# The half swap of the rotary embedding in a hybrid decoder layer: from a matrix product to transfers issued by GpSimd

## The chip, the cores and the metric

The kernel runs on one core of one Trainium2 chip. The metric is the device time of one launch in microseconds. The kernel before took 1616.17 us (median of 3 runs, 1615.53 to 1617.78).

## The reference

One decoder layer over 512 tokens of width 1024: a combined input projection, then two mixing parts side by side (differential attention with a rotary embedding, and an RWKV-7 time mixing), an output projection, and a mixture of experts (top 4 of 32). What matters here is the rotary embedding. Each attention head has two 64-wide parts for the queries and the keys, and each part is turned by an angle per position:

```python
def apply_rope(x, cos, sin):
    c = cos[:, :, None, None, :]
    s = sin[:, :, None, None, :]
    x1, x2 = jnp.split(x.astype(F32), 2, axis=-1)
    return jnp.concatenate([x1 * c - x2 * s, x2 * c + x1 * s], axis=-1).astype(x.dtype)

q = apply_rope(q.reshape(B, S, DA_HEADS, 2, DA_HEAD_DIM), cos, sin)
k = apply_rope(k.reshape(B, S, DA_HEADS, 2, DA_HEAD_DIM), cos, sin)
s = jnp.einsum('bhcqd,bhckd->bhcqk', qi, kt, preferred_element_type=F32) * scale
```

The second term of each half needs the other half of the same vector: 32 values are exchanged with the 32 beside them.

## The kernel before

The program has three parts: `front` (input projection and mixing, up to about 377 us), `output_and_route`, and `experts`. Only `front` is touched. There the features lie on the 128 partitions and the 512 tokens along the free dimension, so that a swap of halves is an exchange of partition blocks: rows 0 to 31 with 32 to 63, and 64 to 95 with 96 to 127.

`front` writes one instruction stream for each engine. The order of each is written out by hand, and engines wait for one another by counting semaphores: `s_out` counts projected tiles that ScalarE has copied to SBUF, and the classes `Steps` (objects `PE`, `AC`, `DV`) count named steps of TensorE, ScalarE and VectorE. The lists `MIX_PE`, `MIX_ACT` and `MIX_DVE` name these steps in order, so a step that is taken out of a stream is taken out of its list.

The mixing loop runs four times, for `j` in 0 to 3, once for each attention head and the pair of RWKV heads beside it; one pass is called a head below. `own_tiles(j)` gives the number `n0` of its first projected tile: tile `n0` holds the queries, `n0 + 1` the keys, `n0 + 2` the values. Beside its mixing, TensorE projects the next head's tiles in pieces (`tile`, L784), except in the last head. What lies around the swap:

- SP (L319) loads weight tiles of 512 KB; each waits for VectorE's split of an earlier one.
- ScalarE copies query and key tiles into `pall` (L384, L467 and L469 of the loop), copies `kappa` and `beta` (L472, L475), and splits a weight tile (L375).
- TensorE computes the products of `beta`, `kappa` and `khat` (L842, L845, L853), the first level products (L861), then the swap: two products with a constant matrix `swap` into banks 7 and 6 (L899, L900). Directly behind it come the level updates (L870, L873), a piece of the next tile, and the level products of level 1 (L861).
- VectorE masks the level products (L658), computes one product for the bonus (L673), the sign on the sine table in head 0 only (L677), the products with the cosines (L680), adds the level update (L666, twice), splits a weight tile except in the last head (L536), then computes the products with the sines from the two banks into `sc` (L686), masks level 1 (L658) and adds the two parts (L690).
- GpSimd computes the angles and writes an empty list to memory (L366) at the beginning; after that it has no work until `front` ends.

`sc` also holds the exponentials of the attention scores (L435) and, in its first columns, squares of the output (L447).

Of the kernel before, what the change touches and what calls it, by code (L numbers as in the profile page):

```python
# [23 lines left out]
ALU = mybir.AluOpType  # L24
# [3 lines left out]
P = 128  # L28
D = 1024
S = 512  # L30
NT = S // P
KT = D // P
IN_TILES = 26
HEADS = 4
CH = 64
# [96 lines left out]
def build_program(nc, d, out):  # L132
    _, at = constant_tables()
    with ExitStack() as top:
# [28 lines left out]
        with ExitStack() as st:  # L163
            front(nc, d, sb, sem, st, dict(cst=cst, cols=cols, stat=stat, o_t=o_t, list_dram=list_dram), con, ident, psum, bank)
# [20 lines left out]
def own_tiles(j):  # L185

    return LEAD + 6 * j


def place_of(n):  # L190
# [1 line left out]
    return n if n < 2 else ORDER[n] // HEADS  # L192


MIX_PE = (["lora_w", "lora_a", "kk_sum", "lora_g", "mb", "t_kappa", "t_beta", "t0_0", "t0_1", "mk", "rope_swap", "x0_0", "x0_1"]
# [19 lines left out]
def front(nc, d, sb, sem, st, g, con, ident, psum, bank):  # L215
# [7 lines left out]
    s_whi, s_wlo, s_prod, s_out = sem("w_hi"), sem("w_lo"), sem("projected"), sem("p_copied")  # L223
    s_zero, s_rope, s_lam1, s_ang = sem("p_zeroed"), sem("rope_steps"), sem("lam_steps"), sem("angles_done")
    s_trig, s_lex, s_lora, s_set, s_set2 = sem("trig_done"), sem("lam_exp"), sem("lora_loaded"), sem("mix_set"), sem("mix_set2")
    s_ready = sem("lora_inputs_ready")
    s_empty, s_emptied = sem("empty_lists_ready"), sem("slot_lists_emptied")
    s_rest, s_part_out = sem("less_and_masks_ready"), sem("own_parts_copied")
    PE = Steps(sem("mix_tensor_steps"), MIX_PE)
    AC = Steps(sem("mix_scalar_steps"), MIX_ACT)  # L230
    DV = Steps(sem("mix_vector_steps"), MIX_DVE)

    pall = sb(st, "pall", [P, 6, S + 1])
    cosb = sb(st, "cosb", [P, S])
    sinb = sb(st, "sinb", [P, S])
# [38 lines left out]
    sc = sb(st, "sc", [P, 2, S])  # L274
# [22 lines left out]
    def tile_of(group, shift=1):  # L297
        return pall[:, group, shift:shift + S]
# [25 lines left out]
    @block.gpsimd  # L324
    def _(pool):
        nc.gpsimd.dma_start(cols[:], d["cols"]).then_inc(s_cols, 16)
        nc.gpsimd.dma_start(posi[:], d["positions"].to_broadcast([P, S])).then_inc(s_pos, 16)
        nc.gpsimd.dma_start(lam[:].rearrange("p a b -> p (a b)"), d["lam"].to_broadcast([P, 256])).then_inc(s_lam, 16)
        nc.gpsimd.memset(zz[:, 0, :], 0.0)
        nc.gpsimd.memset(pe_[:, :, 0:1], 1.0)  # L330
        nc.gpsimd.memset(pall[:, :, 0:1], 0.0).then_inc(s_zero, 1)
        pool.wait_ge(s_zero, 1)

        pool.wait_ge(s_cst, 16)
        pool.wait_ge(s_pos, 16)
        step = 0

        def chain(ins):
            nonlocal step
            step += 1  # L340
            ins.then_inc(s_rope, 1)
            pool.wait_ge(s_rope, step)

        two_pi = 2 * np.pi
        c1 = 6.28125
        c2 = float(np.float32(two_pi - c1) - np.float32(two_pi - c1) % np.float32(2.0 ** -20))
        c3 = float(two_pi - c1 - c2)
        chain(nc.gpsimd.tensor_copy(cosb[:], posi[:]))
        chain(nc.gpsimd.tensor_scalar(sinb[:], cosb[:], con("inv"), None, ALU.mult))
        for dst, shift in ((ang, 0.25), (turns, 0.0)):  # L350

            chain(nc.gpsimd.tensor_scalar(cosb[:], sinb[:], float(1 / two_pi), shift, ALU.mult, ALU.add))
            chain(nc.gpsimd.tensor_scalar(cosb[:], cosb[:], 12582912.0, None, ALU.add))
            chain(nc.gpsimd.tensor_scalar(cosb[:], cosb[:], 12582912.0, None, ALU.subtract))
            for c, angle in ((c1, sinb[:]), (c2, dst[:]), (c3, dst[:])):
                chain(nc.gpsimd.tensor_scalar(taken, cosb[:], -c, None, ALU.mult))
                chain(nc.gpsimd.tensor_tensor(dst[:], taken, angle, ALU.add))
            if shift:
                chain(nc.gpsimd.tensor_scalar(dst[:], dst[:], float(np.pi / 2), None, ALU.add))
            chain(nc.gpsimd.tensor_scalar(dst[:], dst[:], 3.1415925, -3.1415925, ALU.min, ALU.max))  # L360
            pool.sem_inc(s_ang, 1)
        nc.gpsimd.memset(empty, 0.0).then_inc(s_empty, 1)
        pool.wait_ge(s_empty, 1)
        nc.gpsimd.memset(empty[:, :, 0:1], BIG).then_inc(s_empty, 1)
        pool.wait_ge(s_empty, 2)
        nc.gpsimd.dma_start(g["list_dram"].rearrange("(p r) w -> p r w", p=P), empty).then_inc(s_emptied, 16)  # L366
        pool.wait_ge(s_emptied, 16)

    @block.scalar
    def _(act):  # L370
# [162 lines left out]
    def _(dve):  # L533
        def split(n):
            dve.wait_ge(s_whi, n + 1)
            nc.vector.tensor_tensor(w_lo[:, n % 3], w_raw[:, n % 2], w_hi[:, n % 3].bitcast(F32), ALU.subtract).then_inc(s_wlo, 1)  # L536
# [35 lines left out]
        for j in range(HEADS):  # L572
            more = j < HEADS - 1
            n0 = own_tiles(j)
# [106 lines left out]
            level_added(0)  # L681
            if more:
                split(n0 + 3)
            dve.wait_ge(PE.sem, PE.reached(j, "rope_swap"))
            for a, group, dst in rope:
                nc.vector.tensor_tensor(sc[:, group, :], bank(7 - group), sinb[:], ALU.mult).then_inc(DV.sem, DV.step(a + "s"))  # L686
            level_masked(1)
            own("ks")
            for a, group, dst in rope:
# [75 lines left out]
    def _(pe):  # L765
# [27 lines left out]
        for j in range(HEADS):  # L793
            more = j < HEADS - 1
            n0 = own_tiles(j)
# [5 lines left out]
            def dv(name):  # L801
                pe.wait_ge(DV.sem, DV.reached(j, name))

            def ac(name):
                pe.wait_ge(AC.sem, AC.reached(j, name))

            def scores(i):
                n = (i + 1) * P
                for c in range(2):
                    rows = slice(64 * c, 64 * c + 64)  # L810
                    nc.tensor.matmul(bank(6 + c, 0, n), qr[rows, i * P:(i + 1) * P], kro[rows, 0:n], start=True, stop=False)
                for c in range(2):
                    last = nc.tensor.matmul(bank(6 + c, i * P, n), masks[:, 0, :], masks[:, 1, :], start=False, stop=True)
                last.then_inc(PE.sem, PE.step(f"score{i}"))
# [79 lines left out]
            level_products(0, (1,))  # L894
            dv("khat")
            quarters(from_k).then_inc(PE.sem, PE.step("mk"))
            pe.wait_ge(s_out, n0 + 2)
            ac("e_beta")
            nc.tensor.matmul(bank(7), con("swap"), tile_of(0), start=True, stop=True)  # L899
            nc.tensor.matmul(bank(6), con("swap"), tile_of(1), start=True, stop=True).then_inc(PE.sem, PE.step("rope_swap"))  # L900
            level_update(0, 0)
            level_update(0, 1)
            tile(n0 + 2, 2, 5)
# [2 lines left out]
            level_update(1, 1)  # L906
            tile(n0 + 2, 5, 8)
            dv("k")
            scores(0)
            pe.wait_ge(s_out, n0 + 3)  # L910
            turned("v_turn", 4 + (n0 + 2) % 2, lambda t: pall[:, 2, t * P + 1:t * P + P + 1])
# [34 lines left out]
            for h in range(2):  # L946
                for t in range(NT):
                    u = h * NT + t
                    for rows in halves:
                        last = nc.tensor.matmul(bank(2, u * CH, (u + 1) * CH, rows), ak[rows, h, t, 0, :], vt[rows, t, halves[h]],  # L950
                                                start=True, stop=True)
# [5 lines left out]
            for h in range(2):  # L957
                for t in range(NT):
                    for rows in halves:
                        last = nc.tensor.matmul(bank(3 * (1 - h), t * P, t * P + P, rows), xx[rows, h, t, 1, :], rh[rows, h, t, :],  # L960
                                                start=True, stop=True)
# [11 lines left out]
            for t in range(NT):  # L973
# [4 lines left out]
                for h, hs, c, tok in each:  # L978
                    last = nc.tensor.matmul(bank(c, 256 + t * CH, 320 + t * CH, hs), bn[tok, t, hs], wu[tok, h, t, CH:P],
                                            start=False, stop=True)  # L980
# [42 lines left out]
            for t in range(NT):  # L1023
                for h, hs, c, tok in each:
                    last = nc.tensor.matmul(bank(c, t * CH, (t + 1) * CH, hs), zz[hs, 2 * t + c, :], qt[hs, t, tok],
                                            start=False, stop=t == NT - 1)
# [1073 lines left out]
```

## Time and profile before

| | before |
|---|---|
| median of 3 runs | 1616.17 us |
| profiled execution | 1614.44 us |
| its span | 1612.8 us |
| mixing, one whole head | 82 us |
| end of `front` | about 377 us |
| TensorE busy over the span | 1553.0 us (96%) |
| VectorE busy | 1321.4 us (82%) |
| ScalarE busy | 1069.4 us (66%) |
| GpSimd busy | 315.3 us (20%) |

The profile records one execution. PE is TensorE (PEld its weight loads), DVE is VectorE, ACT ScalarE, POOL GpSimd, SP the sync engine. L899 is line 899 of the kernel. An entry "out<-in" names the tensors that an instruction writes and reads, and "[idle before <-releaser]" gives the time for which its engine had nothing to do before it, and the event that ended that. The busy times of TensorE are modelled at their ends: matmuls are pipelined and records overlap, so the cadence is read from starts. The engines' totals cover all stages; the swap lies in one of them, and is read from that stage's own rows.

### The profile page before, as it was taken

What the parts mean: (1) busy time and instruction counts of PE and PEld (TensorE: products, weight loads), DVE (VectorE), ACT (ScalarE), POOL (GpSimd) and SP (SyncE); (2) the same over time, 40 slices, a digit from 0 to 9 for tenths busy, and PEclk for the clock granted to TensorE, in tenths of its full rate; (3) what the DMA queues carried; (4) which work ended last, traced back from release to release, by engine and by line L of the source; (5) the groups of instructions that cost most, each with busy time, mean ns of one, the idle gap of its engine ahead of it and who ended that gap; (6) DMA issues with size and microseconds to landing.
All of it is one profiled execution on the core that took longest, in us unless ns stands there. A gap on an engine that the chain in (4) does not pass through costs nothing.

```text
span 1612.8 us, 27293 instructions
## 1 busy us (share of the span) xinstructions
PE 1553.0 (96%) x10213; PEld 1257.3 (78%) x10214; DVE 1321.4 (82%) x1098; ACT 1069.4 (66%) x1011; POOL 315.3 (20%) x262
## 2 busy tenths in 40 slices
PE   5999999987989999999999999999999999999996
PEld 4677777775868888888888888888888888888885
DVE  5556656555499999999999999999999999999996
ACT  4635353434367877777777777777777777777774
POOL 6200000000145312211211222122222112212210
PEclk9999999997989999999999999999999999999998
DMA  6110101005399999999999999999999999999992
GB/s 191 50 54 27 54 28 44 12 2 200 136 363 388 363 389 382 385 382 380 379 376 372 384 390 375 376 368 375 376 377 384 387 375 372 376 362 384 381 377 112
DMA packets 98189, 463.21 MB, mean 287 GB/s; under 512 B 11136, under 2 KB 37792, under 8 KB 48848
## 3 DMA queue, kind: packets, MB, share of 16 engines
q1 hardware_dynamic: 86032, 429.59, 67.9%
q0 software_dynamic: 12096, 32.75, 7.7%
q8 instruction: 45, 0.74, 0.2%
q14 instruction: 16, 0.13, 0.0%
HBM read 448.51 MB, written 22.69 MB: 292 GB/s over the span
## 4 chain that ended last, share of the span: by engine, by line
PE 74%; DVE 1%; DMA 1%; issue 0%; ACT 0%; DVEq 0%; POOLq 0%
PE psum L1919 29%; PE psum L1922 14%; PE psum L1947 14%; PE psum L1952 7%; PE psum L1317 3%; PE psum L1901 2%; PE psum L1909 2%; PE psum L1935 1%; DVE w_pieces_lo L1741 0%; DMA xg<-h_rows,gath_i 0%; PE psum L2037 0%; PE psum L1333 0%; PE psum L1325 0%; DVE x L1863 0%; DMA w_pieces<-in_w_out 0%
## 5 line engine op out<-in xcount | busy, mean ns | idle before, releaser
L1741 DVE TENSOR_TENSOR w_pieces_lo<-w_pieces,w_pieces_hi 128x2048 fp32r<-128x2048 f32 x384 | 867.3, 2286 | 79.9 <-ACT w_pieces_hi L1605 79.8
L1605 ACT ACTIVATE w_pieces_hi<-w_pieces 128x2048 fp32r<-128x2048 f32 x384 | 736.2, 1919 | 220.7 <-PE psum L1922 156.7
L1919 PE MATMUL psum<-w_pieces_hi,xh 128*128 128x512 f32 x1024 | 284.5, 400 | 0.0
L1919 PE MATMUL psum<-w_pieces_hi,xl 128*128 128x512 f32 x1024 | 274.4, 390 | 0.0
L1922 PE MATMUL psum<-w_pieces_lo,xh 128*128 128x512 f32 x1024 | 274.2, 389 | 0.0
L1919 PEld LDWEIGHTS psum<-w_pieces_hi,xl 128*128 128x128 f32 x1024 | 192.3, 188 | 41.3
L1922 PEld LDWEIGHTS psum<-w_pieces_lo,xh 128*128 128x128 f32 x1024 | 192.2, 188 | 40.2
L1919 PEld LDWEIGHTS psum<-w_pieces_hi,xh 128*128 128x128 f32 x1024 | 185.5, 189 | 45.1 <-issue 11.3
L1545 POOL DMA_INDIRECT sum_rows<-ys,this_i x30 | 114.5, 3815 | 423.8 <-ACT ys L1625 423.5
L1947 PE MATMUL psum<-w_pieces_hi,ah 128*128 128x512 f32 x512 | 158.0, 390 | 0.1
L1947 PE MATMUL psum<-w_pieces_hi,al 128*128 128x512 f32 x512 | 157.7, 389 | 0.0
L1952 PE MATMUL psum<-w_pieces_lo,ah 128*128 128x512 f32 x512 | 136.8, 389 | 0.0
L1947 PEld LDWEIGHTS psum<-w_pieces_hi,al 128*128 128x128 f32 x512 | 96.1, 188 | 20.0
L1952 PEld LDWEIGHTS psum<-w_pieces_lo,ah 128*128 128x128 f32 x512 | 96.1, 188 | 20.0
L1947 PEld LDWEIGHTS psum<-w_pieces_hi,ah 128*128 128x128 f32 x512 | 95.8, 188 | 20.2 <-DVE al L1757 0.5
L784 PE MATMUL psum<-h_hi_sb,w_hi_sb 128*128 128x512 f32 x208 | 88.0, 423 | 0.0
L1535 POOL COPY this_f<-slot_lists_sb 128x1 f32 x30 | 27.7, 922 | 299.3 <-DMA sum_rows<-ys,this_i 295.2
L784 PE MATMUL psum<-h_hi_sb,w_lo_sb 128*128 128x512 f32 x208 | 81.5, 392 | 0.0
L784 PE MATMUL psum<-h_lo_sb,w_hi_sb 128*128 128x512 f32 x208 | 81.3, 391 | 0.0
L1609 ACT ACTIVATE xh<-psum 128x512 fp32r<-128x512 f32 x64 | 37.6, 588 | 41.8 <-PE psum L1901 41.8
L1128 POOL DMA_DIRECT2D w_pieces<-in_ffn_norm_w x1 | 0.6, 554 | 326.1 <-POOLq L163 326.1
L384 ACT ACTIVATE pall<-psum 128x512 f32<-128x512 f32 x14 | 8.3, 595 | 73.4 <-PE psum L784 73.4
(369 smaller groups left out, 1915.1 us busy)
## 6 DMA issues: line engine op xcount, KB each, us to landing
w_pieces<-in_mlp_w SPq DMA_DIRECT2D x384, 1024.0 KB, 7.9
w_raw<-in_w_in SPq DMA_DIRECT2D x26, 512.0 KB, 4.0
w_pieces<-in_w_out SPq DMA_DIRECT2D x8, 512.0 KB, 9.1
sum_rows<-x POOLq DMA_DIRECT2D x5, 512.0 KB, 3.7
chunk_work<-in_x SPq DMA_DIRECT2D x4, 512.0 KB, 5.6
x<-in_x SPq DMA_DIRECT2D x4, 512.0 KB, 13.6
h_rows<-w_pieces POOLq DMA_DIRECT2D x4, 512.0 KB, 3.5
x<-sum_rows POOLq DMA_DIRECT2D x4, 512.0 KB, 11.5
```

Of the source, the lines that this page charges most:

```text
L784: last = nc.tensor.matmul(o, w[:, n % 3, k, :], h[:, k, :], start=k == 0 and m == 0, stop=k == KT - 1 and m == 2)
L1317: last = nc.tensor.matmul(bank(2 * t + c), o[:, k, t * P:(t + 1) * P], w[:, k, c * 512:(c + 1) * 512], start=k == 0 and m == 0, stop=k == ...
L1545: nc.gpsimd.indirect_dma_start(sum_dram, bass.IndirectOffsetOnAxis(this_i[:, 0:1], 0), ys[:], None, compute_op=ALU.add).then_inc(s_scat, 16)
L1605: nc.scalar.activation(hi[:, p % RING], raw[:, raw_slot(b, p)].rearrange("p r n -> p (r n)"), ACT.Copy).then_inc(s_hi, 1)
L1609: nc.scalar.activation(xh[:, 4 * q:4 * q + 4, :].rearrange("p a b -> p (a b)"), bank(from_bank), ACT.Copy).then_inc(s_xh, 1)
L1741: nc.vector.tensor_tensor(lo[:, p % RING], raw[:, raw_slot(b, p)].rearrange("p r n -> p (r n)"), hi[:, p % RING].bitcast(F32), ALU.subtrac ...
L1901: last = nc.tensor.transpose(bank(into, k * P, k * P + P), xg[:, (4 * q + k) * P:(4 * q + k + 1) * P], ident)
L1909: last = nc.tensor.transpose(bank(into, k * P, k * P + P), rows[:, k // 2, k % 2, :], ident)
L1919: nc.tensor.matmul(bank(up_bank(b) + c), a[:, k, :], hi[:, p % RING, c * 512:(c + 1) * 512], start=False, stop=False)
L1922: last = nc.tensor.matmul(bank(up_bank(b) + c), xh[:, k, :], lo[:, p % RING, c * 512:(c + 1) * 512], start=False, stop=k == KT - 1)
L1947: nc.tensor.matmul(bank(into + c), a[:, 2 * p + r2, :], hi[:, p % RING, r2 * D + c * 512:r2 * D + (c + 1) * 512], start=p == 0 and r2 == 0 ...
L1952: last = nc.tensor.matmul(bank(into + c), ah[:, 2 * p + r2, :], lo[:, p % RING, r2 * D + c * 512:r2 * D + (c + 1) * 512], start=False, sto ...
```

## The change

The two products with the swap matrix leave TensorE's stream, and `rope_swap` its list of steps. In their place GpSimd, once per head, waits for the copies of tiles `n0` and `n0 + 1`, and from the second head on for the previous head's last readers of `sc`. It then issues four transfers from `pall` to `sc`, each of 32 partitions by two rows of 512 values, to the partition block beside it. VectorE waits for the count of a new semaphore `s_swapped` instead of TensorE's step, and its products with the sines read and write `sc` in place. TensorE's wait for `e_beta`, which had stood ahead of the swap, now stands ahead of the first scores. GpSimd waits for all transfers at the end.

```diff
-MIX_PE = ([..., "t0_0", "t0_1", "mk", "rope_swap", "x0_0", "x0_1"]
+MIX_PE = ([..., "t0_0", "t0_1", "mk", "x0_0", "x0_1"]
...
+    s_swapped = sem("rope_halves_swapped")
...
         pool.wait_ge(s_emptied, 16)
+        for j in range(HEADS):
+            pool.wait_ge(s_out, own_tiles(j) + 2)
+            if j:
+                pool.wait_ge(DV.sem, DV.reached(j - 1, "a3"))
+                pool.wait_ge(AC.sem, AC.reached(j - 1, f"o_copy{NT - 1}"))
+            for a in range(0, P, CH // 2):
+                b = a ^ (CH // 2)
+                nc.gpsimd.dma_start(sc[a:a + CH // 2, :, :], pall[b:b + CH // 2, 0:2, 1:S + 1]).then_inc(s_swapped, 16)
+        pool.wait_ge(s_swapped, 64 * HEADS)
...
-            dve.wait_ge(PE.sem, PE.reached(j, "rope_swap"))
+            dve.wait_ge(s_swapped, 64 * (j + 1))
             for a, group, dst in rope:
-                nc.vector.tensor_tensor(sc[:, group, :], bank(7 - group), sinb[:], ALU.mult).then_inc(DV.sem, DV.step(a + "s"))
+                nc.vector.tensor_tensor(sc[:, group, :], sc[:, group, :], sinb[:], ALU.mult).then_inc(DV.sem, DV.step(a + "s"))
...
             quarters(from_k).then_inc(PE.sem, PE.step("mk"))
-            pe.wait_ge(s_out, n0 + 2)
-            ac("e_beta")
-            nc.tensor.matmul(bank(7), con("swap"), tile_of(0), start=True, stop=True)
-            nc.tensor.matmul(bank(6), con("swap"), tile_of(1), start=True, stop=True).then_inc(PE.sem, PE.step("rope_swap"))
             level_update(0, 0)
...
             dv("k")
+            ac("e_beta")
             scores(0)
```

## Rows read from the trace of the kernel before

**Rows 1.** Busy time by engine over one whole head, clock, DMA share, GB/s.

```profile
142.00:224.00 82.00, 81.33 (x1131) 61.88 (x1130) 49.15 (x87) 36.12 (x77) 0.00 (x0) 1.00 0.14 40
```

**Rows 2.** Line of the first swap product: duration ns min/median/max, first and last start.

```profile
L899 PE MATMUL psum<-pall,cst x8: 592/644/697, 74.1 to 321.2; 128*128 128x512 f32 x8
```

**Rows 3.** Timeline, TensorE's weight loads, second head: start us, us, instruction, idle before.

```profile
156.32 0.30 PEld L899 LDWEIGHTS psum<-pall,cst 128*128 128x128 f32 x2 [0.17 <-issue]
...
158.24 0.19 PEld L870 LDWEIGHTS psum<-chunk_work 64*64 64x64 f32 x4 [0.76 <-DVE kro L680]
```

**Rows 4.** Timeline of VectorE around the swap in the second head (head 1).

```profile
155.56 0.42 DVE L658 TENSOR_TENSOR chunk_work<-psum,cst 128x256 f32<-128x256 f32 x1 [0.45 <-PE psum L861]
...
157.16 0.69 DVE L680 TENSOR_TENSOR kro<-pall,cosb 128x512 f32<-128x512 f32 x1
159.43 0.69 DVE L666 TENSOR_TENSOR chunk_work<-chunk_work,psum 128x512 f32<-128x512 f32 x1 [1.58 <-PE psum L873]
160.37 0.69 DVE L666 TENSOR_TENSOR chunk_work<-chunk_work,psum 128x512 f32<-128x512 f32 x1 [0.25 <-PE psum L873]
160.97 1.22 DVE L536 TENSOR_TENSOR w_lo_sb<-w_raw,w_hi_sb 128x1024 fp32r<-128x1024 f32 x1
162.11 1.28 DVE L686 TENSOR_TENSOR sc<-psum,sinb 128x512 f32<-128x512 f32 x2
```

**Rows 5.** Timeline of VectorE around the swap in the first head (head 0).

```profile
74.37 0.48 DVE L677 TENSOR_SCALAR sinb<-sinb,cst 128x512 f32<-128x512 f32 x1
...
75.50 0.68 DVE L680 TENSOR_TENSOR kro<-pall,cosb 128x512 f32<-128x512 f32 x1
...
78.18 0.69 DVE L666 TENSOR_TENSOR chunk_work<-chunk_work,psum 128x512 f32<-128x512 f32 x1 [0.25 <-PE psum L873]
...
79.92 1.28 DVE L686 TENSOR_TENSOR sc<-psum,sinb 128x512 f32<-128x512 f32 x2
81.11 0.83 DVE L658 TENSOR_TENSOR chunk_work<-psum,cst 128x256 f32<-128x256 f32 x2
```

**Rows 6.** Timeline of VectorE around the swap in the last head (head 3).

```profile
324.73 0.69 DVE L666 TENSOR_TENSOR chunk_work<-chunk_work,psum 128x512 f32<-128x512 f32 x1 [0.24 <-PE psum L873]
325.34 1.28 DVE L686 TENSOR_TENSOR sc<-psum,sinb 128x512 f32<-128x512 f32 x2
327.62 0.89 DVE L658 TENSOR_TENSOR chunk_work<-psum,cst 128x256 f32<-128x256 f32 x2 [1.00 <-PE psum L861]
```

**Rows 7.** Timeline of ScalarE: the key tile's copy in heads 0, 1 and 3.

```profile
68.06 0.60 ACT L384 ACTIVATE pall<-psum 128x512 f32<-128x512 f32 x1 [2.06 <-PE psum L784]
...
150.25 0.60 ACT L384 ACTIVATE pall<-psum 128x512 f32<-128x512 f32 x1 [2.08 <-PE psum L784]
...
314.62 0.60 ACT L384 ACTIVATE pall<-psum 128x512 f32<-128x512 f32 x1 [2.08 <-PE psum L784]
```

**Rows 8.** Timeline of GpSimd: its last issue in `front`, its first ones afterwards.

```profile
51.31 0.64 POOL L366 DMA_DIRECT2D slot_lists<-o_t  x1 [0.30 <-POOL o_t L364]
...
378.03 0.55 POOL L1128 DMA_DIRECT2D w_pieces<-in_ffn_norm_w  x1 [326.08 <-POOLq L163]
...
379.65 0.53 POOL L1131 DMA_DIRECT2D ffn_norm_cols<-in_ffn_norm_w  x1
```

**Rows 9.** DMA issues of GpSimd: count, KB each, median us from issue to landing.

```profile
xg<-h_rows,gath_i POOLq DMA_INDIRECT x33, 8.3
...
sum_rows<-ys,this_i POOLq DMA_INDIRECT x30, 13.4
...
slot_lists<-o_t POOLq DMA_DIRECT2D x1, 128.0 KB, 3.2
...
ffn_norm_cols<-in_ffn_norm_w POOLq DMA_DIRECT2D x1, 4.0 KB, 7.5
```

**Rows 10.** Timeline of ScalarE: the first head's last use of `sc`.

```profile
125.35 0.36 ACT L447 ACTIVATE sc<-psum,ast 128x128 f32<-128x128 f32 x1
```

**Rows 11.** Line L603 on VectorE: duration ns min/median/max, first and last start.

```profile
L603 DVE SCALAR_TENSOR_TENSOR rkv<-pall,cols,rkv x12: 724/744/894, 49.9 to 307.2; 128x512 f32<-128x512 f32 x12
```

More of the change, by code:

```diff
@@ L192, in place_of @@
     return n if n < 2 else ORDER[n] // HEADS
-MIX_PE = (["lora_w", "lora_a", "kk_sum", "lora_g", "mb", "t_kappa", "t_beta", "t0_0", "t0_1", "mk", "rope_swap", "x0_0", "x0_1"]
+MIX_PE = (["lora_w", "lora_a", "kk_sum", "lora_g", "mb", "t_kappa", "t_beta", "t0_0", "t0_1", "mk", "x0_0", "x0_1"]
           + ["t1_0", "t1_1", "x1_0", "x1_1", "score0", "v_turn"]
```

## The prediction, made before the result was known

> **What bounds the kernel now.** I looked first at the stretches of the mixing stage, because the change touches nothing else. In the 82 us of one whole head TensorE is busy for 81.3 us, VectorE for 49.2 and ScalarE for 36.1, GpSimd for nothing, and the DMA engines for 14% [rows 1]. That is the reading that matters most: in a head TensorE has next to nothing to wait for, so a microsecond taken out of its instruction stream should be a microsecond off the head, unless it hands the path to another engine. GpSimd and the DMA engines, where the work is sent, are free. TensorE's granted clock is 1.00 there, the level of 2.4 GHz, so nothing is lost to the clock that could be won back.
>
> Next I read the order of events around the swap on each engine, in three heads, to learn when its input is ready, when its result is used, and what slack lies between.
>
> **What is removed.** Per head two fp32 products of 128x512. Each shows as two passes: the line of the first product has 8 records over four heads, 592 to 697 ns [rows 2], and the second line is alike. Four such passes would be some 2.4 us, but that is not the saving, because passes overlap. The weight loads give the cadence: in head 1 the first of the swap starts at 156.32 and the first of the level update behind it at 158.24 [rows 3]. So TensorE moves on 1.92 us earlier. The level update's input is ready by then: VectorE's L658 writes it and ends at 155.56 + 0.42 = 155.98 [rows 4]. The note on the row at 158.24 that blames a vector step of the rope is only that of the last event before it; that line of the code waits for nothing of the rope.
>
> **Does VectorE let it through?** Its sequence is: cosine products (L680), first update (L666, twice, each waits for TensorE), the split of a weight tile (L536), sine products (L686), next mask (L658). The cadence of back-to-back 128x512 operations is 0.60 us (L666 at 160.37, L536 at 160.97) [rows 4].
> Head 1: the second L680 starts at 157.16, VectorE is free at 157.76. The first L666 could have its input at 159.43 - 1.92 = 157.51, so it starts at 157.76; the second is free at 158.36, its input comes at 160.37 - 1.92 = 158.45. It starts then, and the full 1.92 us is passed on (with only 0.09 us to spare). Head 2 has the same spacing.
> Head 0 has one more operation (the sign on the sine table), so VectorE is free at 75.50 + 0.60 = 76.10; the two L666 start at 76.10 and 76.70, the second against 78.18 before. Here 78.18 - 76.70 = 1.48 us is passed on, for L686 and L658 follow without a gap (79.92, 81.11) [rows 5]: VectorE, not TensorE, is last at L658.
> Head 3 has no weight split here; its second L666, at 324.73, comes forward by 1.92 as in head 1 [rows 6].
> Sum: 1.48 + 3 x 1.92 = 7.24 us, if the swapped rows are there in time.
>
> **What is added.** GpSimd issues four transfers per head, 32 partitions x 4 KB (128 KB) each, 512 KB in all, once the copy of the second tile is done. VectorE waits for them instead of for TensorE, and queued behind that wait are the sine products, L658 and all further levels, on which TensorE waits in turn. The sine product's form hardly changes: it reads SBUF in place of PSUM, and L680, both operands in SBUF, takes the same 0.69 us as L666 with one in PSUM [rows 4]. I cost that at nothing.
>
> When must the swap have landed? From the end of the second copy (start plus 0.60: 68.66, 150.85, 315.22 [rows 7]) to the brought-forward L686:
> head 0: 79.92 - 1.48 - 68.66 = 9.78 us;
> heads 1 and 2: 162.11 - 1.92 - 150.85 = 9.34 us;
> head 3: 325.34 - 1.92 - 315.22 = 8.20 us, and there L658 had stood idle for 1.00 us waiting for TensorE [rows 6], so 9.20 us.
>
> When does it land? GpSimd is free: its last issue in this stage is at 51.31, and that started 0.30 us after its releaser; consecutive issues lie (379.65 - 378.03) / 3 = 0.54 us apart [rows 8]. I take 0.55, so the fourth is issued at 0.30 + 3 x 0.55 = 1.95 us. From issue to landing no row shows a transfer from SBUF to SBUF. The nearest are 3.2 us for 128 KB out of SBUF in this stage [rows 9], and from above the 7.5 us of the last of four GpSimd issues while the DMA engines were full of other loads [rows 9]. I take 3.2 to 3.5, because the stage's DMA engines are at 14%: a weight load of 512 KB runs beside the first microseconds, no more. So the swap is complete 5.2 to 5.5 us after the copy: 3.8 us to spare at the least. With 7.5 it is 9.45 us: late by 0.11 in heads 1 and 2 and by 0.25 in head 3, half a microsecond in all. The new waits for the previous head's last weights and last output copy cost nothing: that copy ran at 125.35, 25 us before GpSimd needs it [rows 10]. The end wait on GpSimd is over some 50 us before the stage ends. SP's queue is not touched; its loads wait for weight splits, which come forward with the rest. TensorE's wait for the copy of beta moves to just before the scores, many microseconds after that copy.
>
> A rule speaks against the choice of queue. Ahead of the sine product VectorE runs tensor-tensor forms [rows 4]; the only tensor-scalar form is head 0's at 74.37, 5.7 us after that head's copy [rows 5, 7]. The Trainium skill (SBUF — State Buffer, the box "The DVE blocks DMA trap") says that descriptors of a GpSimd DMA cannot be written while VectorE holds the shared port pair in a two-port mode, and that the sync queue is immune; it exempts tensor_tensor. By that rule the sum stays as it is here, and I cannot see it proven by a row.
>
> The Trainium skill (DMA: Bandwidth & Descriptors, "Anatomy of one DMA") fits about 2.0 us plus bytes over 436 GB/s for such a DMA, an estimate of 2.3 us for 128 KB. The measured 3.2 us is used instead.
>
> **The rivals.**
> A. The swap lands late but still pays. If a transfer takes 8.3 us, as the gathers issued by GpSimd do [rows 9], it is complete at 1.95 + 8.3 = 10.25 us: late by 0.47, 0.91, 0.91 and 1.05, together 3.34; gain 3.9 us, 1612.3. For it: the kernel has such landings. Against: those moved scattered rows in a loaded stage. Chance 0.10.
> B. VectorE becomes the bound. It has 0.09 us of spare in heads 1 to 3. If GpSimd's descriptor work stretches VectorE's operations, as L603 ranges from 0.724 to 0.894 us [rows 11], the longest while GpSimd still computed (its arithmetic ends just before 51.31 [rows 8]), then some 11 operations between the copy and the swap's end by 0.17 us each are 1.87, less the 0.45 us for which VectorE waits at L658 anyway [rows 4]: 1.4 us per head. What is left is about 4 x 0.4 = 1.6 us: 1614.6, not to be told from no change. Against: GpSimd's part is four issues, not arithmetic. Chance 0.09.
> C. The four transfers do not overlap: each starts when the one before has landed. Then 0.30 + 4 x 3.2 = 13.1 us, late by 3.32, 3.76, 3.76 and 3.90, together 14.7; less 7.24, 7.5 us slower, 1623.7. The place is VectorE's wait ahead of L686 in each head. It decides against the change from where the lateness sums to 7.24, at 11.2 us after the copy. For it: the transfers share one queue and one semaphore. Against: four GpSimd issues 0.54 us apart, of which the last landed 7.5 us after its own issue [rows 8, 9], which leaves no room for three landings of that length before it. Chance 0.08.
> D. The same wait, but with descriptors held up while VectorE is busy, as long as the 13.4 us of the scatters [rows 9]: 15.35 us, late by 23.7 in all, 16.5 us slower, 1632.7. Against: those scatters ran beside full DMA engines. Chance 0.05.
> That the swap never leaves TensorE is not possible: its products are gone from the stream.
>
> **How the numbers follow.** The likeliest case, chance 0.68, gives 7.24 us. The profiled execution took 1614.44 us (span 1612.8), 1.7 us under the median of the runs, 1616.17; the sum is a difference and is taken from that median: 1616.17 - 7.24 = 1608.9. Its own range is 1607.7 to 1610.5, from TensorE gaining a little more than the cadence (up to 0.3 us per head) to landings of 7.5 us and some stretch. Two in ten may be left out: A and B must come in, C and D stay outside, so 1607.5 to 1616.5 holds 0.87. A measurement of this kernel can tell about 0.2%, 3.2 us, from no change: faster means under 1612.9. The first case and A give 0.78 for faster, B gives 0.09 for the same, C and D 0.13 for slower.
>
> **What the profile of the changed kernel would show.** No products with the swap matrix; the first weight load of the level update directly behind those of khat, and heads about 1.9 us shorter (1.5 in the first). Sixteen GpSimd issues, four per head, 0.55 us apart, starting some 0.3 us after the second copy, each landing in 3 to 4 us. VectorE with no idle time ahead of L686's counterpart; an idle time there, released by a DMA, would show A, C or D, and its length says which. Sine products, or L646 and L649 beside the issues, longer than 0.69 us would show B. TensorE's granted clock should stay at 1.00 in the first three heads. I would be wrong if a transfer between partitions of SBUF is much slower than one out of it, which no row here shows, or if TensorE, freed of 1.9 us, meets a later wait that I have not followed: before, it idled for 0.7 us in 82 [rows 1], so there was none hidden nearby.

## The result and the profile after

The changed kernel took 1607.72 us (median of 5 runs, 1607.04 to 1608.66) against 1616.17 before (5 runs by now, with the same median and range): a ratio of 0.9949, with a 95% interval of 0.9938 to 0.9961, so about 8.2 us faster and between 6 and 10. The forecast was 1608.9, in a range of 1607.5 to 1616.5. The profiled execution took 1607.04 us, span 1605.3 (before: 1614.44 and 1612.8).

The lines of TensorE's weight loads in the second head, which answers to [rows 3] (start us, us, instruction; line numbers are 10 higher in this part):

```profile
155.98 0.25 PEld L863 LDWEIGHTS psum<-kr,khat 64*64 64x64 f32 x6
156.20 0.25 PEld L880 LDWEIGHTS psum<-chunk_work 64*64 64x64 f32 x4
```

The level update's loads stand directly behind those of `khat`: the swap is gone and nothing waits in its place. VectorE in the same head, to be read beside [rows 4]:

```profile
157.25 0.68 DVE L690 TENSOR_TENSOR kro<-pall,cosb 128x512 f32<-128x512 f32 x1
157.85 1.28 DVE L676 TENSOR_TENSOR chunk_work<-chunk_work,psum 128x512 f32<-128x512 f32 x2
159.05 1.22 DVE L546 TENSOR_TENSOR w_lo_sb<-w_raw,w_hi_sb 128x1024 fp32r<-128x1024 f32 x1
160.18 1.28 DVE L696 TENSOR_TENSOR sc<-sc,sinb 128x512 f32<-128x512 f32 x2
```

The idle times of 1.58 and 0.25 us ahead of the two updates are gone, and the sine products (L696) have no idle time ahead of them, so the swap was there. Where it came from, GpSimd's issues in the first, second and last head, and their landings over all 16 (count, KB each, median us from issue to landing):

```profile
70.92 2.18 POOL L376 DMA_DIRECT2D sc<-pall  x4 [19.07 <-ACT pall L394]
...
151.22 2.11 POOL L376 DMA_DIRECT2D sc<-pall  x4 [78.12 <-ACT pall L394]
...
311.58 2.11 POOL L376 DMA_DIRECT2D sc<-pall  x4 [78.07 <-ACT pall L394]
```

```profile
sc<-pall POOLq DMA_DIRECT2D x16, 128.0 KB, 3.8
```

The copies of the key tile, which answer to [rows 7], give the length of a head from start to start:

```profile
69.60 0.60 ACT L394 ACTIVATE pall<-psum 128x512 f32<-128x512 f32 x1 [3.73 <-PE psum L794]
...
150.34 0.60 ACT L394 ACTIVATE pall<-psum 128x512 f32<-128x512 f32 x1 [2.11 <-PE psum L794]
...
230.51 0.60 ACT L394 ACTIVATE pall<-psum 128x512 f32<-128x512 f32 x1 [2.08 <-PE psum L794]
...
310.69 0.60 ACT L394 ACTIVATE pall<-psum 128x512 f32<-128x512 f32 x1 [2.07 <-PE psum L794]
```

| us | before | after | gain |
|---|---|---|---|
| start to the copy in head 0 | 68.06 | 69.60 | -1.54 |
| head 0 to head 1 | 82.19 | 80.74 | 1.45 |
| head 1 to head 2 | 82.17 | 80.17 | 2.00 |
| head 2 to head 3 | 82.20 | 80.18 | 2.02 |
| head 3 to GpSimd's first issue behind `front` | 63.41 | 59.96 | 3.45 |
| together | 378.03 | 370.65 | 7.38 |

The first and the last line hold something that is not the change. In each profile TensorE's granted clock was at 0.5 (1.2 GHz) for one stretch of `front` (leaving out its end, where TensorE idles for 9.8 us in both): in the changed kernel's at 60 us, ahead of anything that was changed, in that of the kernel before at 365 us. The columns of these rows are the stretch, its length, the busy time and instructions of TensorE, its weight loads, VectorE, ScalarE and GpSimd, the granted clock, and the DMA share with GB/s. The first row is of the changed kernel, the second of the one before:

```profile
60.00:63.40 3.40, 3.40 (x7) 1.90 (x6) 1.65 (x3) 3.36 (x6) 0.00 (x0) 0.50 0.00 0
```

```profile
364.60:368.00 3.40, 3.40 (x42) 3.06 (x40) 0.28 (x1) 0.73 (x4) 0.00 (x0) 0.51 0.00 0
```

The one goes with a start that is later by 1.54 us. What the other cost can be read on its own, from the weight loads just ahead of it:

```profile
359.47 0.56 PEld L969 LDWEIGHTS psum<-chunk_work,wu 64*64 64x64 f32 x32 [2.12 <-ACT wu L507]
...
363.68 0.14 PEld L999 LDWEIGHTS psum<-zz,gt 64*64 64x64 f32 x2 [1.76 <-DVE zz L744]
```

The same two loads of the changed kernel start at 353.48 and 357.68. From the key tile's copy in head 3 to the first of them are 44.85 us before and 42.79 after: the last head gains 2.06 us. From the second to GpSimd's first issue are 14.35 and 12.97 us: the stretch at half clock cost 1.4. So the two stretches nearly cancel, and the four heads give 1.45 + 2.00 + 2.02 + 2.06 = 7.5 us. Behind `front` the two profiles differ by another 0.1 us only.

### The profile page after: what moved, and what is told of

The parts are those of the page before. It is cut to its first block, busy times and chain, and to the rows that moved or that the text cites. A ratio compares the mean times of both kernels' runs of the same rounds, so it can differ in the third digit from the quotient of the medians.

```text
span 1605.3 us, 27281 instructions
## 1 busy us (share of the span) xinstructions
PE 1544.0 (96%) x10197; PEld 1253.3 (78%) x10198; DVE 1320.3 (82%) x1098; ACT 1068.9 (67%) x1011; POOL 324.7 (20%) x278
## 4 chain that ended last, share of the span: by engine, by line
PE 74%; DVE 1%; DMA 1%; issue 0%; ACT 0%; DVEq 0%; POOLq 0%
PE psum L1926 29%; PE psum L1929 14%; PE psum L1954 14%; PE psum L1959 7%; PE psum L1324 3%; PE psum L1908 2%; PE psum L1916 2%; PE psum L1942 1%; DVE w_pieces_lo L1748 0%; DMA xg<-h_rows,gath_i 0%; PE psum L2044 0%; PE psum L1340 0%; PE psum L1332 0%; DVE x L1870 0%; DMA w_pieces<-in_w_out 0%
## 5 line engine op out<-in xcount | busy, mean ns | idle before, releaser
L1552 POOL DMA_INDIRECT sum_rows<-ys,this_i x30 | 106.1, 3537 | 421.0 <-ACT ys L1632 420.7
L1542 POOL COPY this_f<-slot_lists_sb 128x1 f32 x30 | 43.7, 1455 | 304.7 <-DMA sum_rows<-ys,this_i 300.4
L376 POOL DMA_DIRECT2D sc<-pall x16 | 8.5, 541 | 253.3 <-ACT pall L394 253.3
```

The costliest lines, as they stand in the source:

```text
L1542: nc.gpsimd.tensor_copy(this_f[:], lists[:, bass.ds(e, 1), 0:1].rearrange("p a c -> p (a c)")).then_inc(s_float, 1)
L1552: nc.gpsimd.indirect_dma_start(sum_dram, bass.IndirectOffsetOnAxis(this_i[:, 0:1], 0), ys[:], None, compute_op=ALU.add).then_inc(s_scat, 16)
```

## The experiments

The theory after the result: the gain is TensorE's shorter stream, passed on by VectorE; the transfers are hidden and free; a late transfer would cost its lateness. The rivals: the transfers cost something, or part of the gain has another source. "The changed kernel" is the base of every edit. Heads are compared by the spacing of the key tile's copies.

**The changed kernel once more.** No edit.

> The changed kernel, unaltered, timed beside the others. Both theories: about 0.995 of before, some 8 us less. What is looked for is the stretch of TensorE's granted clock at 0.5 that the changed kernel's profile has at 60 us, 10 us ahead of the first transfer, and that of before has at 365 us. If it belongs to the change, it is at 60 us again; if it falls where it happens to, it may be at another place or be missing, and then the span of this profile is 1.5 us shorter.

Measured: 1608.5 us, ratio 0.9953 (0.9941 to 0.9966); heads 80.74, 80.22 and 80.20 us apart. The stretch at half clock was again there, from 60.4 us on. That alone looks like the change's doing, but in the other kernels below it began at 58.4 to 61 us in three (products kept, one at a time with TensorE busy, held to the mask) and was absent in six, five of which keep the transfers. So it does not follow from the transfers. That it belongs to the single execution and not to a kernel is not shown: only this kernel was profiled twice, and it had the stretch both times. TensorE stood idle for 2.90 us just ahead of it, and as long in the profile of the kernel before, which kept full clock there. The weight loads that end this idle time, of the changed kernel and of the one before:

```profile
59.10 0.30 PEld L891 LDWEIGHTS psum<-sq,cst 128*128 128x128 f32 x2 [2.90 <-ACT sq L463]
```

```profile
59.22 0.30 PEld L881 LDWEIGHTS psum<-sq,cst 128*128 128x128 f32 x2 [2.90 <-ACT sq L453]
```

So one and the same idle time of 2.9 us was followed by half clock in the profiles of some kernels and not of others. The stretch at 365 us is alike: its two idle times, of 2.12 and 1.76 us, are in all twelve profiles, and 3.4 us of half clock followed in nine of them (not in the two of the changed kernel, nor in that with VectorE's other order).

**Transfers and products.**

```diff
+            pe.wait_ge(s_out, n0 + 2)
+            ac("e_beta")
+            nc.tensor.matmul(bank(7), con("swap"), tile_of(0), start=True, stop=True)
+            nc.tensor.matmul(bank(6), con("swap"), tile_of(1), start=True, stop=True).then_inc(PE.sem, PE.step("rope_swap"))
             level_update(0, 0)
```

> The transfers as in the changed kernel, but TensorE also computes the two products with the swap matrix again, which nobody reads. Theory (all of the gain is TensorE's stream, and transfers and the sine products from SBUF cost nothing): the time of before, 1616 us, within 1.5 us. Rival (the transfers, or reading SBUF in place of PSUM, lengthen VectorE's work): slower than before, by 1 us a head if each of ten operations grows by 0.1 us. Rival (part of the gain came from VectorE no longer waiting for TensorE's step): faster than before by 2 us or more.

Measured: 1616.01 us, ratio 0.9995 (0.9987 to 1.0004), and heads of 82.19, 82.21 and 82.23 us. With the products back, all of the gain is gone, and the transfers and the sine products from SBUF add nothing that shows. In the second head VectorE's updates wait for TensorE again:

```profile
160.24 0.69 DVE L676 TENSOR_TENSOR chunk_work<-chunk_work,psum 128x512 f32<-128x512 f32 x1 [1.58 <-PE psum L883]
161.17 0.69 DVE L676 TENSOR_TENSOR chunk_work<-chunk_work,psum 128x512 f32<-128x512 f32 x1 [0.24 <-PE psum L883]
```

**Neither.** Neither transfers nor products: GpSimd's part of the loop goes, with VectorE's wait for it, and the sine products read the key tile itself.

```diff
-        for j in range(HEADS):
...
-            dve.wait_ge(s_swapped, 64 * (j + 1))
+            if j:
+                dve.wait_ge(AC.sem, AC.reached(j - 1, f"o_copy{NT - 1}"))
-                nc.vector.tensor_tensor(sc[:, group, :], sc[:, group, :], sinb[:], ALU.mult).then_inc(DV.sem, DV.step(a + "s"))
+                nc.vector.tensor_tensor(sc[:, group, :], tile_of(group), sinb[:], ALU.mult).then_inc(DV.sem, DV.step(a + "s"))
```

> Neither products nor transfers: the halves are not swapped, the sine products read the unswapped tile, so this part of the computation is left out. Theory (the transfers are wholly hidden): the time of the changed kernel within 1 us, and heads 1 and 2 80.2 us apart as in it. Rival (the transfers cost something by contention or lateness): faster than the changed kernel by what they cost, up to 1.9 us per head.

Measured: 1607.97 us, ratio 0.9948 (0.9935 to 0.9961); heads 80.72, 80.20 and 80.22 us apart, those of the changed kernel within 0.05. The transfers cost nothing that can be measured, neither on VectorE nor elsewhere. Rival B of the prediction is out.

**One transfer at a time.**

```diff
                 nc.gpsimd.dma_start(sc[a:a + CH // 2, :, :], pall[b:b + CH // 2, 0:2, 1:S + 1]).then_inc(s_swapped, 16)
-        pool.wait_ge(s_swapped, 64 * HEADS)
+                pool.wait_ge(s_swapped, 64 * j + 16 * (a // (CH // 2) + 1))
```

> Each of a head's four transfers is issued only when the one before has landed, which is the rival C of the prediction made on purpose. With 2.8 us a transfer (heads 0 and 3 of the changed kernel's profile) and 4.9 us for those beside a weight load (head 1), plus 0.3 us from a landing to the next issue, the swap is complete 12.4 us after the copy in heads 0 and 3 and up to 16 in heads 1 and 2. Theory (each microsecond past 9.8, 9.3, 9.3 and 9.2 us after the copy is a microsecond lost): late by 2.6, 3 to 6.5 twice, and 3.2, together 12 to 19 us, so 1620 to 1627 us, 4 to 11 over before. Rival (VectorE's wait is covered by other work): no more than 2 us over the changed kernel.

Measured: 1633.09 us (6 runs, 1628.55 to 1637.07), ratio 1.0104 (1.0086 to 1.0122). That is 17 us over before where 4 to 11 were expected, and 25 over the changed kernel. The waits came together to 18.2 us, within the 12 to 19 expected, though that of head 0 was 4.87 and not 2.6: its first and last transfer took 4.3 and 4.1 us, each beside a weight load; the first two heads' and the last's:

```profile
83.33 1.30 DVE L696 TENSOR_TENSOR sc<-sc,sinb 128x512 f32<-128x512 f32 x2 [4.87 <-DMA sc<-pall]
...
169.57 1.29 DVE L696 TENSOR_TENSOR sc<-sc,sinb 128x512 f32<-128x512 f32 x2 [4.52 <-DMA sc<-pall]
...
341.82 1.29 DVE L696 TENSOR_TENSOR sc<-sc,sinb 128x512 f32<-128x512 f32 x2 [3.87 <-DMA sc<-pall]
```

Head 1 to head 2 took 87.37 us, 7.2 more than in the changed kernel, for a wait of 4.52. The missing 2.7 us are in the clock: TensorE, waiting for VectorE's mask, stood idle for 4.91 us, and then ran at half clock.

```profile
171.25 0.29 PEld L880 LDWEIGHTS psum<-chunk_work 64*64 64x64 f32 x4 [4.91 <-DVE chunk_work L668]
```

```profile
160.00:169.00 9.00, 6.49 (x151) 5.61 (x147) 4.62 (x7) 0.00 (x0) 1.60 (x3) 1.00 0.39 104
170.10:176.90 6.80, 5.64 (x69) 5.14 (x70) 5.21 (x10) 0.00 (x0) 0.00 (x0) 0.50 0.01 2
```

The four heads together show 20.5 us at half clock. My theory of the price was incomplete; the next kernels test that.

**The same with TensorE kept busy.**

```diff
             level_products(1)
+            ac("e_beta")
+            for _ in range(22):
+                nc.tensor.matmul(bank(7), w_hi[:, (n0 + 2) % 3, 0, :], h_hi[:, 0, :], start=True, stop=True)
             level_update(1, 0)
```

> The kernel with one transfer at a time (1633 us), with 22 products of 128x512 in each head that nobody reads, placed where TensorE had stood idle for some 5.8 us for the late swap; 22 x 0.227 us are 5.0 us. It tells apart what of that kernel's 25 us over the changed one is lateness and what the clock. VectorE's waits for the transfers there were 4.9, 4.5, 4.9 and 3.9 us, together 18.2. Theory (the idle time of TensorE brought the stretches of half clock, 20.5 us of them in the mixing, and these the rest): waits as before, granted clock 1.00 in heads 0 to 2, and 1607.9 + 18.2 = 1626 us, some 7 under the kernel without them. Rival (the half clock has another cause, or the rest is something else that follows from lateness): 1633 us as before, or more by the added products.

Measured: 1630.0 us (5 runs, 1627.68 to 1633.36), ratio 1.0088 (1.0074 to 1.0101). The median is 3 us below that without the products, not the 7 expected, and the runs of the two overlap; the heads of the profiles decide. In heads 0 and 3 the transfers came sooner this time (waits of 0.89 and 2.25 us), and the added 5.3 us of products were themselves last: these heads are 4.5 and 5.1 us longer than in the changed kernel. Heads 1 and 2 are the clean ones. Each waited 5.49 us, longer than before, and yet they took 85.79 and 85.77 us, less than the 87.37 and 86.66 of the kernel without the products. The granted clock from 72 to 380 us was 1.00, but for a last stretch from 379.3 us on:

```profile
169.44 1.29 DVE L696 TENSOR_TENSOR sc<-sc,sinb 128x512 f32<-128x512 f32 x2 [5.49 <-DMA sc<-pall]
```

```profile
72.00:380.00 308.00, 299.32 (x4285) 232.68 (x4281) 176.34 (x318) 120.48 (x267) 8.02 (x15) 1.00 0.13 36
```

With TensorE busy a wait of 5.49 us goes with a head 5.6 us longer; with TensorE idle one of 4.52 goes with 7.2. The products alone would lengthen a head by some 5 us, so the 5.6 are not the price of the wait alone; what is shown is that TensorE's idle time brought the half clock, since filling it took the half clock away.

**Two at a time.**

```diff
+                if a == CH // 2:
+                    pool.wait_ge(s_swapped, 64 * j + 32)
```

> The second pair of a head's transfers is issued when the first pair has landed. From the changed kernel's landings (2.8 us in heads 0 and 3, up to 4.9 beside the weight load) the swap is complete about 0.3 + 0.55 + 2.8 + 0.3 + 0.55 + 2.8 = 7.3 us after the copy in heads 0 and 3 and about 9.4 us or less in heads 1 and 2, where 9.3 are to be had. Theory (there is slack of that size and nothing is paid within it): within 1.5 us of the changed kernel, 1607 to 1610 us. Rival (one of a head's transfers cannot be late without cost, because something else reads it or the issue itself costs): some 2 us per head more, 1616 us.

Measured: 1608.39 us, ratio 0.9956 (0.9943 to 0.9970), heads 80.72, 80.16 and 80.23 us apart, no idle time ahead of the sine products. In head 1 the last transfer was issued at 156.5 and landed 2.6 us later, 8.9 us after the copy's end; the sine products started at 159.39. In head 2 the swap was complete 9.27 us after the copy, 0.02 us ahead of the sine products. The slack is there, and within it nothing is paid.

**Issues held back.** Two kernels let GpSimd issue only after a later step of VectorE: `et0_1` (the mask) in the one shown, and `kc` (the cosine products) in the other, which has that name in the same line.

```diff
+            pool.wait_ge(DV.sem, DV.reached(j, "et0_1"))
             for a in range(0, P, CH // 2):
```

> The changed kernel, with GpSimd's issues held until VectorE has masked the first level products (156.07 in head 1 of the changed kernel's profile). With 0.3 us to the first issue, 1.6 to the fourth and 2.8 to its landing the swap is complete at 160.8 in head 1, where the sine products start at 160.18: late by 0.6 us in heads 1 and 2, by nothing in head 0 and by 0.8 in head 3. Theory (beyond the slack a microsecond costs a microsecond): 2 us over the changed kernel, 1610 us, no half clock. Rival (any idle time of TensorE brings the half clock): 1.6 us more for each head that is late, 1614 us or more.

> The same, held until VectorE has computed the cosine products (157.93 in head 1): late by 2.4, 2.5, 2.5 and 2.7 us, together 10 us. Theory of lateness alone: 1618 us and granted clock 1.00 in heads 0 to 2. Theory of lateness and clock (TensorE's idle time of about 3 us in each head, against 5.8 in the kernel with one transfer at a time, is enough for a stretch at half clock, which costs 1.6 us for 3.4 us of it): 1.6 us more per head, 1624 us. The two kernels with one transfer at a time leave open which holds at 3 us.

Measured: 1613.26 us, ratio 0.9982 (0.9973 to 0.9991), and 1629.3 us, ratio 1.0079 (1.0065 to 1.0093). The one is 3 us over its theory's 1610 and by the time alone nearer to the rival's 1614; the other is 5 us over 1624. The profiles tell why. GpSimd's first issue came 0.6 to 0.8 us after its releaser, not the expected 0.3, in the last head of both kernels the second issue hung back by a further 0.3, and in the first head of the second kernel landings took up to 4.9 us. VectorE's waits became 0.55, 0.90, 1.17 and 2.42 us in the one (0.93 of the last beside an idle time that VectorE has there anyway) and 4.97, 3.29, 3.34 and 3.99 us in the other. In the first kernel no head has a stretch at half clock, which rules its rival out; the four heads are longer by 0.6 + 1.0 + 1.3 + 1.5 = 4.4 us, about what the waits come to, and a stretch at 365 us, which the changed kernel's profile lacks, makes up most of the rest. In the second the heads are longer by 20.9 us: 14.7 of waits where 10 were expected, and 6.3 of half clock, as the theory of lateness and clock had it. The waits in the second head, of the one and of the other, and TensorE's idle time behind them:

```profile
162.32 1.30 DVE L697 TENSOR_TENSOR sc<-sc,sinb 128x512 f32<-128x512 f32 x2 [0.90 <-DMA sc<-pall]
```

```profile
164.00 0.19 PEld L881 LDWEIGHTS psum<-chunk_work 64*64 64x64 f32 x4 [1.27 <-DVE chunk_work L669]
```

```profile
168.69 1.29 DVE L697 TENSOR_TENSOR sc<-sc,sinb 128x512 f32<-128x512 f32 x2 [3.29 <-DMA sc<-pall]
```

```profile
170.37 0.29 PEld L881 LDWEIGHTS psum<-chunk_work 64*64 64x64 f32 x4 [3.67 <-DVE chunk_work L669]
```

The granted clock of the second one, in the stretches around that idle time:

```profile
150.00:170.50 20.50, 16.74 (x273) 13.54 (x274) 15.81 (x26) 6.06 (x11) 2.11 (x4) 1.00 0.29 78
170.50:173.90 3.40, 3.40 (x64) 3.36 (x64) 2.04 (x4) 0.00 (x0) 0.00 (x0) 0.51 0.03 5
173.90:190.00 16.10, 16.10 (x275) 12.73 (x272) 10.61 (x22) 6.72 (x19) 0.00 (x0) 1.00 0.13 36
```

Head 1 to head 2 in all of them, in us, over the changed kernel's 80.17 us (TensorE's idle time is that of its weight loads ahead of the level update behind the mask):

| kernel | VectorE's wait | TensorE idle | at half clock | head longer by | beyond the wait |
|---|---|---|---|---|---|
| two at a time | 0 | 0.31 | 0 | 0.0 | 0.0 |
| held to the mask | 0.90 | 1.27 | 0 | 1.0 | 0.1 |
| held to the cosines | 3.29 | 3.67 | 3.4 | 5.0 | 1.7 |
| one at a time | 4.52 | 4.91 | 6.8 | 7.2 | 2.7 |
| one at a time, TensorE busy | 5.49 | 0.96 | 0 | 5.6 | 0.1 |

Over all heads of these kernels, TensorE's idle time ahead of the level update was between 0.3 and 1.7 us or between 3.1 and 5.9. The short ones were never followed by a stretch at half clock, the long ones always, 8 of 8. What lies between is open, the one at 59 us of 2.9 us going either way. Nor is the length of one idle time all that counts: near the end of `front` half clock followed idle times of 2.12 and 1.76 us in nine profiles of twelve. The Trainium skill (TensorE: Matmul & The Clock Gate, "HAM oscillation — how this bites in real kernels") warns of this very pattern, waits for data that let the clock fall time and again; the trace agrees, and here each such wait cost 1.4 to 2.7 us on top.

**Issued by SP.** The same waits and the same four transfers, in a helper `swap` that issues them by SP, placed in SP's loop over the weight tiles; GpSimd's loop goes.

```diff
+            if n in (own_tiles(0) + 4, own_tiles(1) + 4, own_tiles(2) + 4):
+                swap((n - LEAD - 4) // 6)
             if n >= 2:
                 sp.wait_ge(s_wlo, n - 1)
```

> The same four transfers per head, issued by SP ahead of that head's weight load, not by GpSimd. Theory (the transfers are hidden, so who issues them does not matter): the time of the changed kernel within 1 us; their landings in heads 1 and 2 are shorter than 4.9 us, since the weight load is behind them and not beside them, and the weight load, some 2 us later, still lands tens of us before its split. Rival (VectorE's work is slowed by GpSimd's issues): faster than the changed kernel. Rival (SP's queue is held up by the swap's waits): slower, with ScalarE waiting for weights.

Measured: 1607.73 us, ratio 0.9950 (0.9936 to 0.9963), heads 80.76, 80.20 and 80.20 us apart. Who issues does not matter. The landings answer the other question:

```profile
w_raw<-in_w_in SPq DMA_DIRECT2D x26, 512.0 KB, 4.0
...
sc<-pall SPq DMA_DIRECT2D x16, 128.0 KB, 2.6
```

In the second and third head they are 2.5 and 2.6 us in the middle, against 4.9 with GpSimd's issues beside the weight load. The Trainium skill (DMA: Bandwidth & Descriptors, "Issuing engines are not separate DMA queues") says that transfers from all engines run on the same 16 DMA engines and interleave, and the trace agrees. This kernel changes the order and the issuing engine at once, but others part the two. With two at a time, GpSimd's first pair of head 1 ran beside the load (150.19 to 154.94) and took 4.8 and 4.7 us, its second pair came behind the load and took 2.6 and 2.6; held to the mask, all four of GpSimd's came behind the load and took 2.6 to 2.9. So the 2 us more were the load of 512 KB, and who issues has no visible share in them.

**VectorE's order.** The sign product of the sine table goes ahead of the first mask, and the product for the bonus moves from ahead of the cosine products to ahead of the first row maxima.

```diff
+            if not j:
+                dve.wait_ge(s_trig, 1)
+                nc.vector.tensor_scalar(sinb[:], sinb[:], con("sign"), None, ALU.mult).then_inc(s_lam1, 1)
             dve.wait_ge(PE.sem, PE.reached(j, "mb"))
...
-            nc.vector.scalar_tensor_tensor(r_, r_, par(j, 7), k_, ALU.mult, ALU.mult).then_inc(DV.sem, DV.step("rk"))
...
+            nc.vector.scalar_tensor_tensor(r_, r_, par(j, 7), k_, ALU.mult, ALU.mult).then_inc(DV.sem, DV.step("rk"))
```

> The changed kernel with VectorE's order changed: the sign on the sine table moves into an idle time ahead of the first mask, and the product for the bonus from ahead of the cosine products to just ahead of the first maximum. Theory (in the changed kernel VectorE, not TensorE, is last at the first level update, by 0.6 us in head 0 and by 0.1 us in heads 1 and 2): head 0 to head 1 shortens from 80.7 to some 80.1 us and the following heads from 80.2 to 80.0 or 80.1, together 0.7 to 1.0 us, 1607 us, within 0.2% of the changed kernel and so to be read from the spacing of heads. Rival (TensorE is last all along): spacings as in the changed kernel.

Measured: 1606.81 us, ratio 0.9946 (0.9932 to 0.9959); heads 80.15, 80.14 and 80.16 us apart against 80.74, 80.17 and 80.18. Head 0 gains the 0.6 us that VectorE had held back, the others 0.03 and 0.02, less than the 0.1 or more expected. The total of 0.6 us can't be told from the changed kernel's by the times, only by the spacing. It is the fastest of all, and in head 0 the updates wait for TensorE again:

```profile
75.20 0.69 DVE L688 TENSOR_TENSOR kro<-pall,cosb 128x512 f32<-128x512 f32 x1
76.07 0.69 DVE L679 TENSOR_TENSOR chunk_work<-chunk_work,psum 128x512 f32<-128x512 f32 x1 [0.18 <-PE psum L883]
77.00 0.69 DVE L679 TENSOR_TENSOR chunk_work<-chunk_work,psum 128x512 f32<-128x512 f32 x1 [0.25 <-PE psum L883]
```

## Why the prediction was right, and where it was not

**TensorE's saving, 1.92 us per head: right, a little low, as the range had allowed.** At the level update TensorE was 158.24 + 0.09 - 156.20 = 2.13 us earlier in head 1 (0.09 is the later start of that head). The cadence from the swap's first load had left out the 0.2 us ahead of it. That all of the gain is TensorE's stream is shown: with the products back it is zero.

**What VectorE passes on, 1.48 + 3 x 1.92 = 7.24: right.** Measured 1.45, 2.00, 2.02 and 2.06, 7.5 us. The "0.09 us to spare" was used up by the 0.2 us more that TensorE offered, so VectorE is last, as the two updates without idle time show; but beyond head 0 only by 0.03 us, as its other order shows.

**From the profile to the median: 7.24 forecast, 7.4 between the profiled executions, 8.2 by the ratio.** The interval, 6 to 10 us, holds all three. What is left over cannot be told from the spread of the runs; stretches at half clock worth about 1.5 us each are in some profiles and not in others.

**The landing, 3.2 to 3.5 us: the mechanism right, the size off both ways.** It was 2.3 to 2.9 us in heads 0 and 3 and 4.7 to 5.6 in heads 1 and 2. The step that failed is "a weight load runs beside the first microseconds, no more": at a DMA share of 14% over the head, the share during those microseconds is another matter. The fourth transfer, issued at 152.80, landed 5.0 us later, so the swap was complete 6.9 us after the copy in head 1, and 7.4 us (232.97 + 5.6 - 231.11) in head 2, not 5.2 to 5.5. Of the slack 2.4 and 1.8 us were left, not 3.8 at the least. The load paid as well: that of head 2 took 6.4 us in place of 4.6, with no wait for it to be seen.

**The time to be had, 9.8, 9.3, 9.3 and 9.2 us: right.** The sine products started 9.78, 9.25 and 9.26 us after the copy in the first three heads. With the swap complete after 9.27 us nothing was lost, and just beyond it the lateness was paid about one for one.

**The price of lateness in rivals A, C and D: wrong beyond 2 us.** C was worked out as 7.5 us slower than before, 1623.7. Made on purpose it took 1633.1. Of the 9.4 us that were missing, the waits explain about 2.5: 17.3 us (18.2 less the 0.9 that the last head covers) in place of 14.7. The rest, some 7 us, is the clock: beyond its wait, head 0 was longer by 87.12 - 80.74 - 4.87 = 1.5 us, head 1 by 2.7, head 2 by 86.66 - 80.18 - 4.90 = 1.6, and head 3 by 1.5, up to the weight load at L976. Of the clock the prediction said only that it was 1.00, could not be won back and should stay so. It should have asked what a wait would do to it. The break-even of 11.2 us after the copy, 1.8 us of lateness per head, lies in the gap that the runs leave open; if the clock falls there, it comes sooner.

**Rival B: out.** VectorE's operations kept their 0.69 us beside the issues, and the kernel without transfers was no faster.

## What to carry to other kernels

A move of work from a full engine to an idle one is worth the instructions' cadence on the full engine, cut down to what the next engine in line lets through; that was right to 4% here by reading starts in one head of each kind. For a transfer that takes the place of a computation, work out the deadline from the last writer of its source to its first reader, and read its landing beside the traffic of those very microseconds, not the stage's mean. And price a missed deadline with what the idle engine does to its clock: here short waits cost themselves, and waits of 3 us and more, with TensorE idle, cost three to six tenths more.

## What the runs showed of the hardware

- In the changed kernel a transfer of 32 partitions x 4 KB from SBUF to SBUF landed 2.7 to 2.9 us after its issue with no load beside it (head 3), and 4.7 to 5.6 us after it beside a load of 512 KB (heads 1 and 2); over all kernels it was 2.2 to 3.6 without a load and up to 6.7 us beside one. In head 0 it went with the time of the load's issue: 2.3 us ahead of the first transfer in the changed kernel, whose transfers took 2.3 to 2.8 us, and 0.7 us ahead of it with VectorE's other order, where they took 4.0 to 4.6. Four issued 0.53 us apart did not wait for one another: in head 3 each landed 2.8 or 2.9 us after its own issue.
- GpSimd's first issue starts 0.3 us after the event that it waits for in heads 1 to 3 of the changed kernel (150.94 to 151.22 in head 1), but 0.7 us after it in head 0 (70.20 to 70.92) and 0.6 to 0.8 us in the kernels that hold it back or issue one at a time. The cause was not looked for; it matters where the slack is small.
- TensorE's idle times of 3.1 to 5.9 us ahead of the level update were followed by half clock in 8 of 8 cases, those of up to 1.7 us in none, and the idle time of 2.9 us at 59 us in some profiles only. Near the end of `front`, idle times of 2.12 and 1.76 us were followed by it in 9 of 12. Products that kept TensorE busy took the half clock away.
- One stretch of 3.4 us at half clock, worth about 1.5 us, is at about 60 us in five profiles of twelve, and was seen in kernels with and without the products, so two profiles can differ by that with no visible cause in the change.
